# First stage of a two-block kernel: order of the loads, of the norm and of the first modulation vector

## The reference, cut to what matters

```python
c_act = silu(c)                                   # (1, 1024)
mod = c_act @ mod_w[0] + mod_b[0]                 # (1, 6144)
sh1, sc1, g1, sh2, sc2, g2 = split(mod, 6)        # 1024 each
u = rms_norm(x, norm_mix[0]) * (1 + sc1) + sh1    # (256, 1024)
q, z_f, v, g = split(u @ a_w_in[0], ...)          # 1024 columns each
f = lb + (1 - lb) * sigmoid(z_f)                  # the forget gate
```

## Time and profile before

| | us |
|---|---|
| median of three runs | 1598.91 |
| the profiled execution: its time | 1588.44 |
| its span, first to last instruction | 1586.5 |
| PE busy | 1489.1 |
| DVE busy | 745.7 |
| ACT busy | 580.9 |
| POOL busy | 28.0 |

### The profile page before, as it was taken

How to read it: one execution, slowest core, us unless ns; L and a number is a source line. 1 busy time by engine, 2 the same in 40 slices (tenths; PEclk the granted TensorE clock), 3 DMA queues, 4 the chain that set the end, 5 groups by cost and what they waited for, 6 DMA issues and landing times.

```text
span 1586.5 us, 26649 instructions
## 1 busy us (share of the span) xinstructions
PE 1489.1 (94%) x11398; PEld 1240.3 (78%) x11398; DVE 745.7 (47%) x1185; ACT 580.9 (37%) x899; POOL 28.0 (2%) x47
## 2 busy tenths in 40 slices
PE   5899999899998989999999899989899999999996
PEld 3898899899998748999999768979666666565653
DVE  3657856776776535554445535653321212122121
ACT  1532234344443445544445735543122222212221
POOL 1000000000001001000000000001000000000000
PEclk8899999999989999999999879999999999999998
DMA  9668735889859503555544223716699999999995
GB/s 328 205 213 286 245 124 197 310 282 322 283 197 353 191 0 127 186 184 179 174 154 133 76 84 107 292 54 216 263 416 425 421 420 424 422 420 425 421 418 211
DMA packets 175635, 404.15 MB, mean 255 GB/s; under 512 B 5013, under 2 KB 139442, under 8 KB 163250
## 3 DMA queue, kind: packets, MB, share of 16 engines
q1 hardware_dynamic: 173504, 397.43, 67.7%
q0 software_dynamic: 1648, 5.18, 1.1%
q10 hardware_dynamic: 386, 0.11, 0.0%
HBM read 401.63 MB, written 1.07 MB: 254 GB/s over the span
## 4 chain that ended last, share of the span: by engine, by line
PE 81%; DMA 8%; DVE 7%; ACT 3%; issue 1%; SPq 0%; DVEq 0%; ACTq 0%
PE ps L1785 28%; PE ps L2303 12%; PE ps L2016 7%; PE ps L2325 6%; PE ps L1820 4%; PE ps L1798 3%; PE ps L2290 3%; DMA late<-in_w 2%; DMA arena<-in_w 2%; PE ps L1949 2%; PE ps L2048 2%; PE ps L2336 2%; PE ps L1873 2%; DMA arena<-in_mod_w 2%; PE ps L1883 2%; DVE wsplit L1134 1%
## 5 line engine op out<-in xcount | busy, mean ns | idle before, releaser
L1785 PE MATMUL ps<-u,wsplit 128*128 128x256 f32 x3912 | 484.8, 285 | 9.3 <-DVE wsplit L1134 7.9
L1785 PEld LDWEIGHTS ps<-u,wsplit 128*128 128x128 f32 x3912 | 476.5, 193 | 16.8 <-DVE wsplit L1134 9.1
L1134 DVE TENSOR_TENSOR wsplit<-arena,wsplit 128x1024 fp32r<-128x1024 f32 x258 | 312.6, 1224 | 249.9 <-ACT wsplit L747 246.9
L747 ACT ACTIVATE wsplit<-arena 128x1024 fp32r<-128x1024 f32 x258 | 270.5, 1056 | 330.4 <-PE ps L1785 153.4
L2303 PE MATMUL ps<-arena 128*64 128x256 f32 x1408 | 156.9, 380 | 5.6 <-DMA arena<-in_w 4.8
L2303 PEld LDWEIGHTS ps<-arena 128*64 128x64 f32 x1408 | 101.3, 137 | 66.7 <-issue 14.2
L2016 PE MATMUL ps<-hid,wsplit 128*128 128x256 f32 x1056 | 130.2, 283 | 0.3 <-DVE hid L1375 0.3
L2016 PEld LDWEIGHTS ps<-hid,wsplit 128*128 128x128 f32 x1056 | 128.2, 192 | 0.5 <-DVE hid L1375 0.5
L1691 DVE TENSOR_TENSOR arena<-arena,ps 128x256 f32<-128x256 f32 x32 | 13.5, 422 | 244.2 <-ACT arena L1093 244.2
L1098 ACT ACTIVATE arena<-ps 64x512 f32<-64x512 f32 x64 | 37.8, 591 | 145.4 <-PE ps L2325 144.6
L1798 PE MATMUL ps<-u,wsplit 128*128 128x256 f32 x528 | 72.1, 299 | 15.0 <-DVE u L1183 13.2
(11 more groups left out here) (349 smaller groups left out, 1421.9 us busy)
## 6 DMA issues: line engine op xcount, KB each, us to landing
arena<-in_w SPq DMA_DIRECT2D x66, 2048.0 KB, 24.9
late<-in_w SPq DMA_DIRECT2D x30, 2048.0 KB, 25.4
arena<-in_mod_w SPq DMA_DIRECT2D x48, 1024.0 KB, 6.6
arena<-in_ffn_w_in SPq DMA_DIRECT2D x44, 1024.0 KB, 5.5
arena<-in_ffn_w_out SPq DMA_DIRECT2D x22, 1024.0 KB, 5.0
arena<-in_a_w_in SPq DMA_DIRECT2D x16, 1024.0 KB, 7.8
arena<-in_kv_mod_w SPq DMA_DIRECT2D x8, 1024.0 KB, 5.9
arena<-in_kv_w SPq DMA_DIRECT2D x8, 1024.0 KB, 7.5
```

The source lines that it names most:

```text
L747: act.activation(piece_buf(p, 0), piece_src(p), ACT.Copy).then_inc(hi_done, 1)
L1134: dve.tensor_tensor(piece_buf(p, 1), piece_src(p), piece_buf(p, 0).bitcast(F32), ALU.subtract).then_inc(lo_done, 1)
L1785: mm = pe.matmul(o, w_[:, k, :], u[:, x_, k, :], start=first, stop=last)
```

## The change

What it does, all of it before the first linear layer:

- The first 2048 columns of `mod_w[0]` are loaded as eight slots of 128 whole rows each (`rows_first`, 8 KB a partition) and no longer as eight slots of 256 columns (1 KB runs). PE takes each with four matmuls of 512 columns into four partition groups of bank 6, and `columns` turns the sum in place of `column(0)`.
- In the list of loads the first `zf` slot stands between the seventh and the eighth of these.
- PE turns `x` at once after `c`, takes rows 0 and 1, makes `sums`, rows 2 and 3, `spread`, row 4, turns the small vectors, takes rows 5 and 6, `warm` 4, row 7, `warm` 2, `columns`, `warm` 3, then the linears.
- DVE makes the masks and `fold` first, then copies `h`, takes the reciprocal of the root, copies the vectors, makes `lbs`, splits two pieces, and only then `mod`, `gain` and the operand. ACT squares and takes the root ahead of `lbs`, splits two pieces, copies the rows' sum, and goes on to the operand.
- POOL's three memsets wait for the end of the first operand as well.
- The later groups of the `gemv` kind are numbered anew (same banks as before); `rows_sb` counts one more.

The diff, cut to its core:

```diff
-    gemv("gemv_first", "mod0", 8)
-    linear("zf", "a_in", D, 4, "act")
+    def rows_first(k):
+        s = slot("rows_first", "mod0", 0)
+        s["k"] = k
+        return s
+
+    jobs["rows_first"] = [rows_first(k) for k in range(DC - 1)]
+    linear("zf", "a_in", D, 1, "act")
+    jobs["rows_first"].append(rows_first(DC - 1))
+    linear("zf", "a_in", D + 256, 3, "act")
...
+                    elif old["kind"] == "rows_first":
+                        sp.wait_ge(first_mm, old["k"] + 1)
...
             pool.wait_ge(setup_c, 4)
+            pool.wait_ge(u_lo, 8)
             pool.memset(GS, 1.0).then_inc(a_init, 1)
...
+            squares("mix0", h, lambda n: (setup_c, 1 + min(n, 3) // 2))
+            root("mix0")
             act.wait_ge(setup_c, 5)
             act.activation(lbs[:, 3, :], lbs[:, 0, :], ACT.Exp).then_inc(act_order, 1)
-            squares("mix0", h, lambda n: (setup_c, 3 + min(n, 3) // 2))
-            gemv_rows(0)
-            root("mix0")
-            hi_upto(LOOKAHEAD)
+            hi_upto(1)
+            act.wait_ge(first_mm, DC)
+            act.activation(gsb[:].rearrange("p a n -> p (a n)"), ps[:, 6, :], ACT.Copy).then_inc(rows_sb, 1)
             operand_hi("mix0", lambda c_: mod[:, c_:c_ + 1], None)
...
+            dve.wait_ge(const_done, 6)
...
+            for b in range(2):
+                dve.wait_ge(setup_t, 1 + b)
+                dve.tensor_copy(h[:, 4 * b:4 * b + 4, :], acc[:, 4 * b:4 * b + 4, :]).then_inc(setup_c, 1)
+            norm_rstd("mix0")
+            dve.wait_ge(setup_t, 3)
+            dve.tensor_copy(vec1[:], ps[:, 0, 0:112]).then_inc(setup_c, 1)
+            dve.wait_ge(setup_t, 4)
+            dve.tensor_copy(vec2[:], ps[:, 1, 0:ROWS2]).then_inc(setup_c, 1)
...
+            lo_upto(1)
             dve.wait_ge(gemv_col, 1)
...
             dve.wait_ge(mod_done, 2)
-            norm_rstd("mix0")
-            lo_upto(LOOKAHEAD)
             operand("mix0", h, lambda c_: gain[:, 0, c_:c_ + 1], lambda c_: mod[:, c_:c_ + 1])
...
+            def first_rows(some):
+
+                for s in some:
+                    pe.wait_ge(slot_in[s["n"] % RING], slot_use(s["n"]))
+                    for g in range(4):
+                        mm = pe.matmul(ps[32 * g:32 * g + 32, 6, :], cact[:, s["k"], 7:39],
+                                       slot_dst(s)[:, 512 * g:512 * (g + 1)], start=(s["k"] == 0),
+                                       stop=(s["k"] == DC - 1), skip_group_check=True)
+                    mm.then_inc(first_mm, 1)
...
-            pe.wait_ge(act_order, 1)
-            gemv(jobs["gemv_first"][:4])
-            pe.wait_ge(ld_vec, 16 * 21)
-            pe.transpose(ps[:, 0, 0:112], rows1[0:112, :], ident[0:112, 0:112]).then_inc(setup_t, 1)
-            pe.transpose(ps[:, 1, 0:ROWS2], rows2[0:ROWS2, :], ident[0:ROWS2, 0:ROWS2]).then_inc(setup_t, 1)
             pe.wait_ge(ld_x, 16)
...
-            gemv(jobs["gemv_first"][4:])
-            pe.wait_ge(folded, 1)
-            column(0).then_inc(gemv_col, 1)
+            pe.wait_ge(act_order, 1)
+            first_rows(jobs["rows_first"][0:2])
             sums("mix0")
+            first_rows(jobs["rows_first"][2:4])
             spread("mix0")
-            pe.wait_ge(setup_c, 2)
+            first_rows(jobs["rows_first"][4:5])
+            pe.wait_ge(ld_vec, 16 * 21)
+            pe.transpose(ps[:, 0, 0:112], rows1[0:112, :], ident[0:112, 0:112]).then_inc(setup_t, 1)
+            pe.transpose(ps[:, 1, 0:ROWS2], rows2[0:ROWS2, :], ident[0:ROWS2, 0:ROWS2]).then_inc(setup_t, 1)
+            first_rows(jobs["rows_first"][5:7])
+            pe.wait_ge(setup_c, 4)
+            warm(jobs["zf"][0:2], 4)
+            first_rows(jobs["rows_first"][7:8])
+            warm(jobs["zf"][0:2], 2)
+            columns(gsb[:].rearrange("p a n -> p (a n)"), 1, modps[:, 0:16]).then_inc(gemv_col, 1)
+            warm(jobs["zf"][0:2], 3)
             linears(jobs["zf"] + jobs["q"], (u_lo, 0))
```

More of the change, by code:

```diff
@@ L304, in two_blocks @@
         acc = ps[:, 2:6, :].rearrange("p b (c t) -> p (b c) t", t=T)
-        gps = lambda group: ps[:, 6 + group % 2, 0:256]
+        gps = lambda group: ps[:, 7 - group, 0:256]
         modps = ps[:, 6, 256:368]
@@ L320, in two_blocks @@
         mod_done = sem("mod_done")
+        first_mm = sem("first_mm")
+        mask_made = sem("mask_made")
         rows_done = sem("rows_done")
@@ L347, in slot_src @@
             w = matrices[s["matrix"]]
-            if s["kind"] == "rows":
+            if s["kind"] in ("rows", "rows_first"):
                 return w[P * s["k"]:P * (s["k"] + 1), s["at"]:s["at"] + 2048]
@@ L757, in gemv_rows @@
                 act.wait_ge(gemv_mm, 8 * group + 8)
-                act.activation(gsb[:, group % 2, :], gps(group), ACT.Copy).then_inc(gemv_sb, 1)
+                act.activation(gsb[:, group, :], gps(group), ACT.Copy).then_inc(gemv_sb, 1)
             def root(name):
@@ L850, in _ @@
                 if r % 4 == 3:
-                    gemv_rows(1 + r // 4)
+                    gemv_rows(r // 4)
             table_of(ACT.Sqrt)
@@ L1209, in add_gated @@
                     ins.then_inc(lin_out["dve"], 1)
[L1212 to L1218, removed]
+            dve.wait_ge(const_done, 6)
+            si, ti, xi = (xor_i[:, n, :] for n in range(3))
+            dve.tensor_tensor(xi.bitcast(I32), si.bitcast(I32), ti.bitcast(I32), ALU.bitwise_xor).then_inc(mask_made, 1)
+            dve.tensor_tensor(si, ti.bitcast(I32), si.bitcast(I32), ALU.is_lt).then_inc(mask_made, 1)
+            dve.wait_ge(mask_made, 2)
+            dve.tensor_copy(ti, xi.bitcast(I32)).then_inc(mask_made, 1)
+            dve.wait_ge(mask_made, 3)
+            dve.scalar_tensor_tensor(out=xi, in0=si, scalar=1000.0, in1=ti, op0=ALU.mult, op1=ALU.add).then_inc(mask_made, 1)
+            dve.wait_ge(mask_made, 4)
+            dve.tensor_scalar(masks[:, 0, :], xi, 0.0, None, ALU.is_equal).then_inc(mask_made, 1)
+            for n, H in enumerate(LEVELS):
+                dve.wait_ge(mask_made, 5 + 2 * n)
+                dve.tensor_scalar(ti, xi, float(H), None, ALU.is_ge).then_inc(mask_made, 1)
+                dve.wait_ge(mask_made, 6 + 2 * n)
+                dve.scalar_tensor_tensor(out=masks[:, n + 1, :], in0=xi, scalar=float(2 * H), in1=ti,
+                                         op0=ALU.is_lt, op1=ALU.mult).then_inc(mask_made, 1)
             dve.tensor_reduce(out=fold[:], in_=ident[:].rearrange("p (g j) -> p j g", g=4)[:, 0:8, :], axis=AX,
                               op=ALU.add).then_inc(folded, 1)
+            for b in range(2):
[6 more added lines that the diff above has]
+            dve.tensor_copy(vec2[:], ps[:, 1, 0:ROWS2]).then_inc(setup_c, 1)
             lb_col = vec2[:, VEC["a_lb"]:VEC["a_lb"] + HA]
@@ L1828, in column @@
                 pe.wait_ge(gemv_sb, group + 1)
+                first = 16 * (group + 1)
                 for m in range(2):
-                    mm = pe.matmul(modps[:, 16 * group + m:16 * group + 16:2], gsb[:, group % 2, P * m:P * (m + 1)],
+                    mm = pe.matmul(modps[:, first + m:first + 16:2], gsb[:, group, P * m:P * (m + 1)],
                                    fold[:], start=True, stop=True)
@@ L1956, in _ @@
                     pe.wait_ge(mod_done, 1)
-                    column(1)
+                    pe.wait_ge(folded, 1)
+                    column(0)
                 gemv(jobs[f"gemv_round{r}"][0:1])
@@ L1966, in _ @@
                 round_(r)
-            column(2).then_inc(gemv_col, 1)
+            column(1).then_inc(gemv_col, 1)
             pe.wait_ge(a_dec, 16)
@@ L2027, in ffn_pe @@
                         pe.wait_ge(mod_done, 3)
-                        columns(gsb[:].rearrange("p a n -> p (a n)"), i // 4,
+                        columns(gsb[:].rearrange("p a n -> p (a n)"), 1 + i // 4,
                                 modps[:, 32 + 4 * i:48 + 4 * i]).then_inc(gemv_col, 1)
@@ L2137, in late_columns @@
                 if i == 2:
-                    columns(late_rows[:, 0, :], 3, ps[:, 0, 0:16])
-                    columns(late_rows[:, 1, :], 3, ps[:, 0, 16:32]).then_inc(gemv_col, 1)
+                    columns(late_rows[:, 0, :], 4, ps[:, 0, 0:16])
+                    columns(late_rows[:, 1, :], 4, ps[:, 0, 16:32]).then_inc(gemv_col, 1)
             attention_pe("B", lambda i, k: half(kB, i), lambda i, k: half(qB, i),
```

## The result

| | before | changed |
|---|---|---|
| median of 19 runs each, us | 1597.96 | 1584.22 |
| lowest and highest | 1586.14, 1605.97 | 1573.15, 1595.49 |
| span of the profiled execution | 1586.5 | 1585.7 |
| first linear pair: start, length | 50.56, 7.48 | 36.09, 6.28 |

The ratio is 0.9916, with a 95% interval of 0.9892 to 0.9940: 13.4 us less (9.6 to 17.3).

The account below looks back on a forecast made before the run. PE was taken as the bound from 54 us on, so the first pair's start counts: 13.3 us earlier plus 1.2 from the pair, 14.5, less 0.5, gives 14.0; 1598.9 - 14.0 = 1584.9 us, range 1580.5 to 1593.

Parts of the forecast that it names:

- The bound: From 54 us on PE is the bound; what the first stage gives back moves the end one for one.
- The loads: Ahead of the first pair: row slots land every 2.5 us, the last row at 28.9 to 31.0 us.
- PE's queue: PE starts the last row between 28.9 and 35.3 us, depending on its clock; 32.0 taken.
- From the last row to the pair: Last row's matmuls to first linear pair: 5.3 us at full clock; the pair 6.27 us for 7.48.
- The memsets: POOL's three memsets, now beside DVE's splits of pieces 2 and 3: cost taken as 0, 5 us at most.
- The 0.5 I had set aside for pieces 2 and 3: Behind the first pair: later splits of pieces 2 and 3 cost between 0 and 0.5 us; 0.5 taken off.
- The number: Whole kernel: 14.0 us less than 1598.9, so 1584.9 us.
- a profile of about 1574: Profiled execution of the changed kernel: about 1574 us, as before's profiled execution lay 10.5 below its median.
- PE is late: Rival, 0.18: PE stays at half clock, last row starts at 33 to 35.3 us; gain 6.6 to 10 us.
- Long runs gain nothing: Rival, 0.10: first-stage slots still take 3.0 us each, pair starts at 38.2 to 40.3; 1585.5 to 1587.5 us.
- The vectors are late: Rival, 0.06: PE waits for small vectors ahead of rows 5 to 7, pair at 47 to 54.3; 1595 to 1602.6 us.
- The memsets block the splits: Rival, 0.08: POOL's memsets hold up splits, up to 5 us of PE's wait in second and third piece; 1590 us.

Follow-up runs that it names:

- e2: Kernel before with only the loads changed to whole rows in 8 KB runs, every engine's order old; timed 1594.49 us, ratio 0.9977 to before.
- e1: Changed kernel with its new order but the old loads of 256 columns in 1 KB runs; timed 1587.52 us, ratio 0.9948 to before.
- e4: Changed kernel without POOL's added wait for the end of the first operand; one profiled execution, first pair at 37.29 us; not timed alone.
- t3: Timed runs of e1's kernel (new order, old 1 KB loads), with a profile: median 1587.52 us of 12 runs, ratio 0.9948 to before.
- e7: Changed kernel with sums, root and spread behind `columns`, as before the change; one profiled execution, first pair 6.4 us later.
- e5: Changed kernel without the nine `warm` matmuls; one profiled execution, first pair starts 1.7 us and ends 3.6 us later.
- e8: Changed kernel with DVE's two splits between `gain` and the operand; one profiled execution, first pair 2.4 us later.

## Why the prediction was right, point by point

- **The bound.** That the first pair's start moves the end one for one fits the medians: 14.5 us earlier, 15.7 with the pair's own 1.2, 14.9 behind the gap of 0.8, and 13.4 (9.6 to 17.3) and 15.3 (9.8 to 21.1) in time. At the same landmark e2's kernel is 4.1 and 4.8 us ahead of before, for 3.7 in time, and e1's 11.6 and 10.3, for 8.3. The intervals are wide, so a loss of a few us on the way is not excluded.
- **The loads.** 28.9 to 31.0 us for the last row; measured 30.92. The rate was right: rows 0 to 5 landed every 2.5 us, row 5 at 21.38 for 20.9. The 2.1 us by which the sum for before was short, taken over as the upper end of this range without a reason, came again. They are the late engine told above: the first engine had the last row at 28.75, and the last one at 30.88.
- **PE's queue: the term that was mis-sized.** I put the last row at 32.0 because I weighed PE at half clock (35.3) against the loads. PE reached full clock by its first row, right behind the turns of `x`, and from there to 30 us it was at half clock for 6.8 us; the sums took 3.73, and PE waited. Even at half clock it waited: 2.35 us ahead of the last row in e4 (sums 4.95) and 3.04 in t3 (sums 6.99). I had read "half clock through 10 to 20 us" as a property of that kind of matmul. It goes with what stood ahead: rows 0 to 3 took 1.94 us each in e2, which turns `x` behind them, and rows 0 to 2 took 1.07 in e7, which turns it first, with PE idle between the rows in both.
- **From the last row to the pair.** Expected 5.3, measured 5.2; the pair 6.27 and 6.28. e5 shows what the `warm` matmuls carry of it.
- **The parts.** Undone one by one: the norm's place 6.4 (e7), the long runs 3.3 (e1), the two splits' place 2.4 (e8). The two splits that are no longer ahead at all were 2.3 more (4.63 for four, 2.36 for two). Together 14.4 of 14.5. That they add up so closely is luck: the long runs are 5.0 in the old order and 3.3 to 4.7 in the new, and e7's last row came 1.3 us early.
- **The memsets.** I took 0 because the splits have two inputs. The splits were indeed not held up (1.2 us each), but I had overlooked the next operation of DVE, which has one tensor input: 2.02 us for 0.4, and 0.8 on PE. The 0.5 I had set aside for pieces 2 and 3 did not come: PE went from the pair into them without a gap (42.29). (Its terms also add up to 7.9 us, 5.7 + 1.0 + 1.2, and not to 8.1.) The two errors nearly cancel.
- **The number.** Median for median it is 13.7 us, for 14.0. By the landmarks the terms came to 14.9. So the forecast is 0.9 short of its own kind of sum, and the scatter of the times hides it. The step to "a profile of about 1574" was wrong: it took for granted that the profiled execution of the changed kernel would lie as far under its median as that of before. It took 1587.78 us, 3.6 over its median.
- **The rivals.** "PE is late": out, PE idled before the last row. "Long runs gain nothing", with the page's 358 GB/s: 415 GB/s and e1 speak against it. "The vectors are late": they came late, at 19.7, in time by less than 2 us; I had let a small load wait six times as long among 8 KB runs, and it was twice. "The memsets block the splits": they block something else, and cost 0.8 us for the 5 at most.

In the Trainium skill, "DMA: Bandwidth & Descriptors", section "Queues, rings and completion order", an engine drains 9 to 17 descriptors of a queue before it turns to the next. By that a small load would let a whole row slot pass each time, eight runs; the packets above, 0.32 us apart, let one run pass. The Trainium skill's page on SBUF ("SBUF — State Buffer", section "SBUF: two separate sides") says that a GpSimd operation and a DVE operation in a two-port mode shut each other out for the whole instruction, while a DVE operation with two SBUF inputs waits only for a GpSimd operation that reads SBUF. The trace agrees for the splits beside memsets (1.2 us). L1278 and, in e4, L1261 were held until a memset's end (47.14 and 46.99 us; 27.10 and 27.07), as the page has it for the two-port mode; which mode an operation ran in, no trace here shows.

## What to carry to other kernels

Ahead of the first dense stretch, write down for every engine what its work needs, not where it stands: here the norm needed only `x` and the splits only a weight, and by e1 moving them beside the loads was worth 11 of 14.5 us, the faster loads 3.3. When such a step is moved, look also at the first thing that each engine does behind it: one forgotten DVE operation beside a memset gave back 0.8 us. Where a load lands later than its bytes account for, look at how far apart its engines finish, and at what else one of them carried. And where single executions spread over 20 us with the clock, judge a change of 10 us by its landmark in the trace and by medians of many runs, not by two spans.

## What the runs showed of the hardware

- 16 matmuls of one column (32 records), back to back for 7 us, stayed at half clock from start to end in before and in e2 (6.96 us, granted 0.50) and in t3 (6.99). Begun at full clock, behind the turns of `x` and two rows, they took 3.73 us in the changed kernel. At full clock later in before, eight records took 0.95.
- Of a load on 16 DMA engines the last engine finished 0.3 to 1.0 us behind the first, and 1.6 to 2.1 us behind it in the slot that was loading when one engine carried 16 KB of instructions for 1.0 to 1.3 us (fourteen traces).
- Small loads beside queued runs of 8 KB: one packet each 0.32 us, one long run between two. The last of 21, issued by 9.7 us, landed at 19.2 us; among runs of 1 KB at 14.1 us.
- A DVE operation with one tensor input and per-partition scalars (128x256) is held up by a POOL memset as one with constants is: 2.02 us for 0.41. A DVE operation with two tensor inputs (128x1024) was not: 1.2 us beside a memset.
- The same kernel spreads over 22 us (1573.15 to 1595.49), in step with the mean granted clock (0.971 to 0.955). Fourteen profiled executions had 84 to 135 us at half clock behind the first stage, and 0.39 us more span for each of these.
